# Feed-forward gate and up products in two halves of 256 tokens, each half with its own weight load

## What is computed

```python
h = rmsnorm_2(x, g_pre_ffn[l]) * (1.0 + sc_f) + sh_f
f = (jax.nn.silu(h @ w_gate[l]) * (h @ w_up[l])) @ w_down[l]
x = x + gt_f * rmsnorm_2(f, g_post_ffn[l])
```

## Time and profile before

| | us |
|---|---|
| median of 2 runs | 3204.07 (3203.84 to 3204.29) |
| profiled execution, first to last instruction | 3201.8 |
| PE busy | 3156.7 (99%) |
| PE weight loads busy | 2603.3 (81%) |
| DVE busy | 1723.7 (54%) |
| ACT busy | 916.3 (29%) |

### The profile page before, as it was taken

The page is one execution under the profiler, slowest core; times in us unless marked ns, Lnnn a source line. Parts: engine busy times, 40 slices in busy tenths (PEclk is TensorE's granted clock), DMA queues, the critical chain, the costliest instruction groups (busy, mean ns, idle before and its releaser), DMA issues.

```text
span 3201.8 us, 38265 instructions
## 1 busy us (share of the span) xinstructions
PE 3156.7 (99%) x14744; PEld 2603.3 (81%) x14744; DVE 1723.7 (54%) x2260; ACT 916.3 (29%) x1124; POOL 268.9 (8%) x414
## 2 busy tenths in 40 slices
PE   8999999999999999999998999999999999999998
PEld 7888877888878888888777888888888888888887
DVE  6666665868874445556788643333333333323354
ACT  5333343223233333444522221111121121121213
POOL 1111100111100000000013220000000000000013
PEclk9999999999999999999998999999999999999999
DMA  5444455766742222222564642322322223222354
GB/s 185 142 132 133 127 187 215 289 255 230 259 190 79 84 87 79 80 79 79 225 251 169 240 133 92 111 93 100 110 92 101 102 98 105 98 98 102 124 179 163
DMA packets 93449, 455.83 MB, mean 142 GB/s; under 512 B 19744, under 2 KB 20016, under 8 KB 56112
## 3 DMA queue, kind: packets, MB, share of 16 engines
q1 hardware_dynamic: 51776, 298.08, 26.4%
q0 software_dynamic: 37696, 128.52, 11.2%
q10 hardware_dynamic: 3888, 28.03, 2.3%
HBM read 421.81 MB, written 26.22 MB: 140 GB/s over the span
## 4 chain that ended last, share of the span: by engine, by line
PE 96%; DVE 3%; DMA 0%; ACT 0%; DVEq 0%; issue 0%; SPq 0%; ACTq 0%
PE PS L1076 24%; PE PS L1078 24%; PE PS L1077 24%; PE PS L1478 5%; PE PS L1477 5%; PE PS L1476 5%; PE PS L1345 1%; PE PS L1372 1%; PE PS L1129 1%; PE PS L1130 1%; PE PS L1131 1%; PE PS L1360 1%; PE PS L1242 0%; PE PS L1201 0%; DVE WL L1523 0%; PE PS L1224 0%
## 5 line engine op out<-in xcount | busy, mean ns | idle before, releaser
L1076 PE MATMUL PS<-XH,WH 128*128 128x512 f32 x3312 | 1298.0, 392 | 5.8 <-DVE WL L1523 2.8
L1078 PE MATMUL PS<-XH,WL 128*128 128x512 f32 x3312 | 1289.0, 389 | 0.0
L1077 PE MATMUL PS<-XL,WH 128*128 128x512 f32 x3312 | 1288.8, 389 | 0.0
L1523 DVE TENSOR_TENSOR WL<-RAW,WH 128x2048 fp32r<-128x2048 f32 x266 | 609.5, 2292 | 498.8 <-ACT WH L680 498.7
L680 ACT ACTIVATE WH<-RAW 128x2048 fp32r<-128x2048 f32 x266 | 509.0, 1914 | 1242.8 <-PE PS L1078 875.4
L1076 PEld LDWEIGHTS PS<-XH,WH 128*128 128x128 f32 x3312 | 621.7, 188 | 145.8 <-issue 13.5
L1078 PEld LDWEIGHTS PS<-XH,WL 128*128 128x128 f32 x3312 | 621.7, 188 | 130.1
L1077 PEld LDWEIGHTS PS<-XL,WH 128*128 128x128 f32 x3312 | 621.8, 188 | 129.6 <-issue 2.2
L1476 PE MATMUL PS<-WH,FH 128*128 128x512 f32 x704 | 273.9, 389 | 0.0
L1477 PE MATMUL PS<-WL,FH 128*128 128x512 f32 x704 | 273.9, 389 | 0.0
L1478 PE MATMUL PS<-WH,FL 128*128 128x512 f32 x704 | 273.9, 389 | 0.0
(11 more groups left out here) (320 smaller groups left out, 2299.9 us busy)
## 6 DMA issues: line engine op xcount, KB each, us to landing
RAW<-w_units_dram SPq DMA_DIRECT2D x268, 1024.0 KB, 4.8
ADA<-w_ada_dram POOLq DMA_DIRECT2D x192, 512.0 KB, 5.5
spill_dram<-SIG POOLq DMA_DIRECT2D x24, 256.0 KB, 2.3
BB<-x_t_dram ACTq DMA_DIRECT2D x1, 4096.0 KB, 15.8
x_dram<-RES ACTq DMA_DIRECT2D x1, 4096.0 KB, 14.9
BB<-x_dram ACTq DMA_DIRECT2D x4, 1024.0 KB, 7.9
x_dram<-BB ACTq DMA_DIRECT2D x4, 1024.0 KB, 5.1
X3T<-x3t_dram ACTq DMA_DIRECT2D x4, 1024.0 KB, 4.9
```

The source lines that it names most:

```text
L1076: pe.matmul(PS[:, bank, :], wh, rh[:, x, :], start=k == 0, stop=False)
L1077: pe.matmul(PS[:, bank, :], wh, rl[:, x, :], start=False, stop=False)
L1078: ins = pe.matmul(PS[:, bank, :], wl, rh[:, x, :], start=False, stop=k == n - 1)
L1523: v.tensor_tensor(WL[:, slot, :], RAW[:, slot, :], f32(WH[:, slot, :]), ALU.subtract)\
```

## The change

The units of the gate and up products are issued by a new function, halved, in place of unit. It makes the same waits and sums the same products into the same bank, but each of the three matmuls of a tile is issued twice, for tokens 0 to 255 and for tokens 256 to 511, and each of the two loads the weight tile for itself. The first chunk's pair and third and all down units stay as they are.

```diff
             FULL = [(k, k) for k in range(TILES)]
 
+            def halved(n, slot, o, bank, x0):
+
+                pe.wait_ge(lo_ready, n + 1)
+                pe.wait_ge(out_read, READ0 + o - 3)
+                for x in range(TILES):
+                    pe.wait_ge(x_ready, x0 + x + 1)
+                    for w, r in ((WH, XH), (WH, XL), (WL, XH)):
+                        for h in range(2):
+                            ins = pe.matmul(PS[:, bank, h * S // 2:(h + 1) * S // 2], w[:, slot, x * P:(x + 1) * P],
+                                            r[:, x, h * S // 2:(h + 1) * S // 2],
+                                            start=x == 0 and w is WH and r is XH and h == 0,
+                                            stop=x == TILES - 1 and w is WL, skip_group_check=True)
+                ins.then_inc(out_done, 1)
+
             def unit(n, slot, o, lists, bank0, banks, x0, rh=XH, rl=XL, last_use=False):
...
                 for k in range(3 if first else 0, 2 * FF_CHUNK):
-                    unit(u + k, k % 2, o + k, [FULL], k % 4, 4, X_FFN)
+                    halved(u + k, k % 2, o + k, k % 4, X_FFN)
```

## The result

| | before | after |
|---|---|---|
| median, us | 3204.07 | 3297.61 (3296.93 to 3298.28) |
| profiled execution, us | 3201.8 | 3295.3 |
| ratio | | 1.029, 95% interval 1.027 to 1.031 |

The change makes the kernel 93.5 us slower. The time lies inside the range on record (3188 to 3310), but not at its likeliest value, 3259. It falls, to a microsecond, on the rival called "load and stream get in each other's way", 3297. The prediction gave 0.67 to a time within 2% of before and 0.32 to one more than 2% slower; the measured one is 2.9% slower. The time was made by the term that was forecast and by one that was costed at nothing.

A forecast was written before the change was run, and what follows sets the result against it. PE was taken as the bound, through the distance between matmul starts. 4080 matmuls, each becoming two halves at 120.1 ns instead of one at 226.7 ns, add 55 us to 3204.1: 3259 us, range 3188 to 3310.

The forecast's parts named there:

- load and stream get in each other's way: Gate and up halves start 124.8 ns apart, 93 us slower; chance 0.27, shared with a short instruction feed.
- The bound: PE bounds the kernel: busy 99% of the span, 96% of the chain, never waiting in the changed stretch.
- growth ahead of both splits: Idle time ahead of ACT's and DVE's weight splits must grow by about what the span grows.
- The distance of 120.1 ns: Time between starts of 256-column halves in gate and up: 106.7 + 13.4 ns.
- The three terms (stream, load floor, remainder): Per half: 106.7 ns streaming 256 columns, at least 111.4 ns between weight loads, 13.4 ns that is neither.
- toll per matmul: Each gate and up half pays the 13.4 ns again: 120.1 ns apart, 55 us slower; chance 0.45.
- per column: The 13.4 ns belong to the columns streamed in gate and up: halves 113.35 ns apart, change 0; chance 0.20.
- The sum of 55 us: Whole forecast change: 4080 gate and up matmuls, each 13.5 ns longer as two halves.
- Edits costed at nothing: Waits, ACT and DVE splitting, DMA, bank reads and handing PE two instructions every 120 ns were taken to add no time.
- a feed of instructions at 125 ns a pair: Handing PE its instructions limits the halves near 125 ns a pair, about 93 us; within a shared chance of 0.27.
- a low clock throughout: Clock at level 0.50 makes a pair of halves cost 427 ns, 816 us slower; chance 0.02.
- Bare loads: The 4080 new weight loads overlap no stream, 111.4 ns each, 455 us slower; chance 0.03.

The follow-up runs named there:

- the loop kept short: The changed kernel with the 8 halved units of chunks 1 to 9 as an inner loop of 2 turns over 4 units: 3258.0 us.
- the unrolled run: The changed kernel with PE's loop over chunks 1 to 9 written out in full, no backward branch: 3258.7 us.
- the loop of 1580: The changed kernel with units 4 to 7 at 512 columns in every chunk but the first, about 1580 instructions a turn: 3264.5 us.

## Why the prediction was right, and where it was wrong

- *The bound.* Right: PE holds 95% of the chain after, and what DVE has left grew by what PE lost (idle ahead of its weight split 417.8 to 483.4 us, ahead of its FV product 245.9 to 273.7, together 93 us). The sign named, growth ahead of both splits, was too narrow: ahead of ACT's split the idle time grew by 28 us only (718.8 to 747.1), and by 66 ahead of its Silu (376.2 to 442.3). The clock was not 0.9 to 1.0 in every slice of the earlier trace rows: one of the 40 reads 8, before the chunks, and nothing hangs on it.
- *The distance of 120.1 ns.* Right: 120.0 measured. The three terms (stream, load floor, remainder) each showed in a shape of their own. The 0.45 and 0.20 between a toll per matmul and per column fell on the right side, but the reason given, that the load takes the toll, is not confirmed.
- *The sum of 55 us.* Right as a term, 53.7 us measured with the loop kept short; wrong as the change of the kernel. It put the kernel within 2% of before, the case given 0.67, and that did not come.
- *The step that failed: "Edits costed at nothing".* It weighed the new instructions by the rate at which PE takes them and found nothing. That is right (the unrolled run). It did not weigh them by their place and length: 768 more instructions in a hardware loop of 1200. The row that could have warned stood on the page, 57 packets of 16 KB: 57 x 256 = 14600 instructions fetched where PE alone carried out 2 x 14744. Loops were being run from memory, and the prediction never asked how large one may get. The missed term is 39 us, 42% of the change. By two of the prediction's own signs, that PE waits and that the clock drops, it was wrong. That the time lies inside the range all the same is luck: the range was as wide as the rivals made it, and none of them was this.
- *The rival at 3297 us* had the measured time and 0.27 of the chance, and nothing of its mechanism: matmuls of 128 columns start 111.8 ns apart, not 125. Its other half, a feed of instructions at 125 ns a pair, fails by the 120 ns between halves; PE did run out of instructions, but only behind a backward branch. A time that agrees with a story is no evidence for it; only the distance between starts told them apart.
- *The clock.* The prediction gave 0.02 to a low clock throughout, rightly: it is 1.00 over 120 us of halves. It fell all the same, for 30 us in all, behind gaps of 2 to 3 us. Nowhere did the prediction price a stall as the idle time plus the low clock behind it.
- *Bare loads.* Out, as forecast: 120 ns holds a load and a stream of 107 ns.

## What to carry to other kernels

Halving the moving operand of a one-pass float32 matmul with a full weight load costs a fixed 13 ns per extra matmul at full clock. Below about 235 columns (an estimate: 111.4 - 13.4 = 98 ns of stream) the weight load becomes the bound. Before adding instructions to a hardware loop, count those of a turn and look at the instruction queue's packets: a loop that was run from memory and no longer fits is fetched anew at each branch, and where its first instruction lands decides whether that costs about 1 us or nearly 5 a branch. Here a turn of some 1390 instructions stayed in memory and one of some 1580 did not. An inner loop, or writing the loop out, takes the loss away at once.

## What was not expected of the hardware

- Fetching code in order is free for PE even at two instructions every 120 ns (125 packets, no wait). A jump back to code that has been dropped shows a gap of about 1 us behind 512-column matmuls (0.6 to 1.3 from start to start), and a further one of 2.2 to 3.1 us if the next packet begins within a few instructions.
- Moving a loop by 96 instructions, without touching it, changed the time by 35 us in 3300.
- Gaps of 2 to 3 us in an otherwise full PE brought 3 to 7 us at half clock behind some branches and not behind others: 7 and 8 of 8 in two profiles of the changed kernel, 2 of 8 in the one with the loop of 1580.
- A load of fewer weight columns did not shorten the distance of 512-column matmuls. It lengthened it, from 226.7 ns to between 230 and 232 ns.
